# Delta rule: a chunk's preparation moved to the end of the step before, and VectorE's side work moved between two marks of each level

## The chip, the cores and the metric

One Trainium2 chip, one of its cores. The program is one launch that computes a whole two-part network block. The metric is device microseconds of one execution; a run's figure is the median of several executions.

## What is computed

The kernel is a long chain of stages (a first block with three mixers and a feed-forward, then two layers with retrieval of experts). The change touches one stage alone, the gated delta rule of the first of these two layers. Cut to what matters, per chunk and head, in both directions of time:

```python
def step(S, inp):                      # one chunk of one head
    qc, kc, vc, gc, bc = inp
    gc = jnp.cumsum(gc, axis=-1)
    decay = jnp.exp(jnp.where(incl, gc[..., :, None] - gc[..., None, :], -jnp.inf))
    kk = jnp.einsum('bhid,bhjd->bhij', kc, kc)
    a = eye + jnp.where(strict, kk * decay * bc[..., :, None], 0.0)
    sol = lax.linalg.triangular_solve(a, rhs, left_side=True, lower=True, unit_diagonal=True)
    u, w = sol[..., :dv], sol[..., dv:]
    v_new = u - w @ S
    o = (qc * jnp.exp(gc)) @ S + (incl * (qc @ kc.T) * decay) @ v_new
    S = S * jnp.exp(g_last) + (kc * jnp.exp(g_last - gc)).T @ v_new
    return S, o
```

There are 16 value heads of width 128 and 512 positions (256 of the context, 256 of the sequence). At the end each head's output is normalized by its root mean square and multiplied by a gain.

## The kernel before, in words

**Work.** The kernel takes chunks of 128 positions and four heads at a time: four groups of heads by four chunks are 16 pieces, k = 0 to 15. A piece is a tile of 128 by 512 (four heads side by side). Both directions are held in one matrix per head, forward below the diagonal, backward above. For each piece there are three jobs:

- **Preparation** (`pe_prep`, `act_prep`, `pool_prep`, `dve_prep`). Two DMAs bring rows of cumulated gates (E and F). ScalarE subtracts them from the column (`differences`, 4 instructions for each direction, L2027), VectorE takes the larger (`pr.min`, L2052), ScalarE the exponential, TensorE four small products of k and q into a bank (`pr.k`, L2007 and L2008), VectorE multiplies (`dve_products`, L2076 for AT, L2078 for the other). GpSimd masks AT to blocks of 8 (`prod`, L2042). VectorE sums them (L2085 through the helper L221) and scales and spreads them (L2089, L2093, `dve_block`); TensorE sends them to all partitions (L2015, `in.ab`); VectorE inverts the 8 by 8 blocks by substitution (`dve_substitute`: seven pairs of L2107 and L2109 in parts 0 to 2; part 3 is L2113, L2114 and L2118, the first W).
- **Inverse** (`pe_inverse`, `act_inverse`, `pool_inverse`, `dve_inverse`): four levels double the block from 8 to 128. A level is transpose W (PE L2134), R = masked transpose (DVE L2165, two halves), y = N R (PE L2142), T = scaled copy (ACT L2185, four heads), x = T B (PE L2150), W = W - x (DVE L2171, two halves). N and B are masked copies that GpSimd makes (L2197, L2204). After the last level GpSimd cuts W into two triangles (L2229, `in.XT`).
- **Recurrence** (`pe_recur` and so on): carry (DVE L2338, four instructions a direction, after PE L2291), vn (PE L2300), its copies on ScalarE, the output (PE L199, added by DVE L2346 or copied by ACT), the state (PE L2321, DVE L2356 or L2353), and for the last piece of a group the norm (DVE L2361 and L2362, one pair per chunk). `pool_stage` does triangles (L2229), Q (L2259) and the scaled v (L2264) a step ahead of it.

**Order.** Each engine has a program of its own, in order, written by hand with semaphores. `chunks` runs 18 steps; in step k the inverse of piece k, the preparation of piece k+1, the stage work of k-1 and the recurrence of k-2 stand side by side. Each of these is a generator with 13 rounds, r = 0 to 12, and `paced` takes one round of each in turn, the inverse first. Rounds 3n, 3n+1 and 3n+2 hold level n: the transpose and R are in the first, y and T in the second, x and W in the third; round 12 holds no level. So whatever an engine is given in round 3n stands behind R there, and whatever it is given in round 3n+2 stands behind W and ahead of the next R. The z projection (`pe_zstep`, L2459: eight matmuls of 512 columns a step, spread by the table `Z`) fills TensorE beside them; its result is copied out by ScalarE in round 12 and stored by the SP queue, which then issues the rows for Q (`sp_queries`, L1962).

**Banks.** The eight PSUM banks go round in a queue (`Banks`): `take` hands out the bank that was given back longest ago and waits for what was named when it was given back.

**VectorE before.** Preparation: r 1 `pr.min`; r 4 and 5 the two products; r 6 and 7 the block work; r 9 to 12 the four parts of the substitution. Recurrence: r 1 and 2 the two carries; r 5 and 6 the outputs; r 7 and 8 the states; for the last piece of a group norms in r 3, 4, 11 and 12. An instruction made with `v()` waits for the preceding one of its engine.

A piece with `st` = (k-2) % 4 = 0 in the recurrence has no carry, one with `st` = 3 has no state but the norms; outputs are added on VectorE at `st` 1 and 3. In steps of k % 4 = 2, 3, 0, 1 the recurrence is at `st` 0, 1, 2, 3.

## Time and profile before

| | |
|---|---|
| median of 3 runs | 4194.38 us (4189.41 to 4195.66) |
| the profiled execution's own time | 4192.27 us |
| its span in the profile | 4190.5 us |
| busy: PE, DVE, ACT, POOL | 83%, 63%, 32%, 29% of the span |
| steps 0 to 15 of the delta rule | 1264.27 to 1760.49 us, 496.2 us |
| its first W ready, its end | 1264.27 us, about 1794.4 us |

Times inside the trace are counted from the start of the span. "DVE" is VectorE, "ACT" ScalarE, "POOL" GpSimd, "PE" TensorE. A step is counted here from the end of one L2118 (the first W of a piece) to the end of the next; the four levels and the last part of the substitution for the next piece lie in it.

### The profile page before, as it was taken

What the parts mean: (1) busy time and instruction counts of PE and PEld (TensorE: products, weight loads), DVE (VectorE), ACT (ScalarE), POOL (GpSimd) and SP (SyncE); (2) the same over time, 40 slices, a digit from 0 to 9 for tenths busy, and PEclk for the clock granted to TensorE, in tenths of its full rate; (3) what the DMA queues carried; (4) which work ended last, traced back from release to release, by engine and by line L of the source; (5) the groups of instructions that cost most, each with busy time, mean ns of one, the idle gap of its engine ahead of it and who ended that gap; (6) DMA issues with size and microseconds to landing.
All of it is one profiled execution on the core that took longest, in us unless ns stands there. A gap on an engine that the chain in (4) does not pass through costs nothing.

```text
span 4190.5 us, 38888 instructions
## 1 busy us (share of the span) xinstructions
PE 3490.2 (83%) x11382; PEld 1850.7 (44%) x11382; DVE 2644.0 (63%) x5552; ACT 1356.8 (32%) x3747; POOL 1210.7 (29%) x1228
## 2 busy tenths in 40 slices
PE   7888978999877888879989887877788787877877
PEld 2344435844335666666544432322233365322222
DVE  3756454858766776545788469677555445887444
ACT  1232120003433455412334333433333232433333
POOL 0001100000005565502343433433444101443332
PEclk9889989999989999989999999999999998999999
DMA  5523314653421112055999999999999714999998
GB/s 219 201 81 137 125 63 169 222 199 134 190 82 33 53 57 62 23 231 201 407 399 409 399 414 419 402 421 421 408 414 420 289 62 175 416 421 408 418 421 362
DMA packets 169765, 1088.29 MB, mean 260 GB/s; under 512 B 16432, under 2 KB 45488, under 8 KB 51152
## 3 DMA queue, kind: packets, MB, share of 16 engines
q0 software_dynamic: 112608, 820.04, 47.7%
q1 hardware_dynamic: 56944, 265.77, 17.2%
q8 instruction: 90, 1.47, 0.1%
q14 instruction: 123, 1.01, 0.1%
HBM read 1075.19 MB, written 10.55 MB: 259 GB/s over the span
## 4 chain that ended last, share of the span: by engine, by line
PE 31%; DVE 27%; DMA 18%; issue 12%; POOL 7%; ACT 4%; DVEq 0%; POOLq 0%; ACTq 0%; SPq 0%
PE bank L199 20%; DMA arena<-in_uv,arena 16%; POOL arena L3023 6%; DVE arena L3040 6%; ACT arena L211 3%; PE bank L2991 3%; DVE arena L443 2%; PE bank L1620 2%; DVE arena L561 2%; DVE arena L217 1%; DVE arena L2109 1%; DVE arena L221 1%; PE bank L2459 1%; DMA arena<-in_w_rows 1%; DVE arena L216 1%
## 5 line engine op out<-in xcount | busy, mean ns | idle before, releaser
L2991 PE MATMUL bank<-arena 128*128 128x512 f32 x3072 | 1491.2, 620 | 353.3 <-ACT arena L211 350.6
L211 ACT ACTIVATE arena<-arena 128x1 f32<-128x1 f32 (+5 forms) x2639 | 872.5, 331 | 2003.9 <-DVE arena L3040 1127.7
L199 PE MATMUL bank<-arena 128*128 128x256 f32 (+4 forms) x4640 | 1299.3, 439 | 73.1 <-ACT arena L211 36.1
L3040 DVE CUSTOM_DVE_ANT_0 arena<-arena 128x1024 f32<-128x1024 f32 x768 | 942.0, 1227 | 609.5 <-DMA arena<-in_uv,arena 571.2
L3023 POOL DMA_INDIRECT arena<-in_uv,arena x768 | 794.9, 1035 | 1251.0 <-PE bank L2991 812.5
L2991 PEld LDWEIGHTS bank<-arena 128*128 128x128 f32 x3072 | 547.5, 192 | 1269.5 <-ACT arena L211 818.6
L199 PEld LDWEIGHTS bank<-arena 128*128 128x128 f32 (+2 forms) x4640 | 804.1, 195 | 556.5 <-issue 427.3
L211 ACT ACTIVATE arena<-bank 128x512 f32<-128x512 f32 (+4 forms) x306 | 160.7, 525 | 481.4 <-PE bank L199 322.6
L443 DVE CUSTOM_DVE_ANT_0 arena<-arena 128x1024 f32<-128x1024 f32 x192 | 240.7, 1254 | 33.9 <-DMA arena<-in_w_rows 22.3
L626 POOL TENSOR_SCALAR arena<-arena 128x1 f32<-128x1 f32 (+3 forms) x48 | 16.9, 351 | 664.7 <-ACT arena L211 471.1
L561 DVE SCALAR_TENSOR_TENSOR arena<-bank,arena 128x508 f32<-128x508 f32 (+2 forms) x248 | 159.0, 641 | 8.8
L211 ACT ACT_TABLE_LOAD x92 | 118.0, 1283 | 78.1 <-DMA arena<-gates_rest 26.3
L217 DVE TENSOR_SCALAR arena<-bank,arena 128x256 f32<-128x256 f32 (+3 forms) x162 | 84.0, 519 | 90.0 <-PE bank L520 48.3
L2185 ACT ACTIVATE arena<-bank,arena 128x128 f32<-128x128 f32 x256 | 73.0, 368 | 208.4 <-PE bank L2142 208.0
L2459 PE MATMUL bank<-arena 128*128 128x512 f32 x256 | 130.2, 611 | 0.0
L2204 POOL TENSOR_TENSOR arena<-arena 128x512 f32<-128x512 f32 x64 | 81.3, 1270 | 91.9 <-DVE arena L2171 46.7
L216 DVE TENSOR_SCALAR arena<-bank,arena 128x256 f32<-128x256 f32 (+5 forms) x98 | 55.4, 565 | 81.0 <-PE bank L199 63.2
L2197 POOL TENSOR_TENSOR arena<-arena 128x512 f32<-128x512 f32 x64 | 81.3, 1270 | 54.2 <-PE bank L2142 50.4
L2171 DVE TENSOR_TENSOR arena<-arena,bank 128x256 f32<-128x256 f32 x128 | 48.2, 418 | 76.3 <-PE bank L2150 72.6
L221 DVE TENSOR_REDUCE arena<-arena 128x32 f32<-128x512 f32 (+10 forms) x99 | 66.2, 669 | 40.2 <-ACT arena L211 34.7
L2134 PE MATMUL bank<-arena 128*128 128x128 f32 x256 | 43.7, 293 | 55.0 <-DVE arena L2118 52.4
L1620 PE MATMUL bank<-arena 128*128 128x512 f32 x176 | 77.4, 602 | 2.7 <-DVE arena L1638 2.7
(255 smaller groups left out, 2599.3 us busy)
## 6 DMA issues: line engine op xcount, KB each, us to landing
arena<-in_w_rows SPq DMA_DIRECT2D x50, 1024.0 KB, 5.0
arena<-in_w_in SPq DMA_DIRECT2D x16, 2048.0 KB, 7.9
arena<-in_wq SPq DMA_DIRECT2D x14, 2048.0 KB, 8.4
arena<-in_dn_w SPq DMA_DIRECT2D x12, 2048.0 KB, 10.0
arena<-in_w_up SPq DMA_DIRECT2D x11, 2048.0 KB, 8.0
arena<-in_dn_wo SPq DMA_DIRECT2D x8, 2048.0 KB, 11.2
arena<-in_w_rows POOLq DMA_DIRECT2D x14, 1024.0 KB, 6.1
arena<-decay_rest SPq DMA_DIRECT2D x56, 256.0 KB, 5.0
```

Of the source, the lines that this page charges most:

```text
L199: t = p.e.matmul(out, l, r, start=(i == 0), stop=(i == n - 1))
L211: return a().activation(out, in_, f, **kw)
L216: return v().tensor_scalar(out, a, s1, None, op0)
L217: return v().tensor_scalar(out, a, s1, s2, op0, op1)
L221: return v().tensor_reduce(out, a, AX, op)
L443: v().tensor_tensor_reduce(trash, w[:, j, :], self.crow[r], 1.0, 0.0, ALU.mult, ALU.add, self.M[m][:, j0 + j, c:c + 1]).then_inc(*(V.up("m ...
L561: t = v().scalar_tensor_tensor(dst[:, :, o], src[:, :, f], wc(d + h), dst[:, :, o], ALU.mult, ALU.add)
L1620: t = p.e.matmul(bs[n], m["act"][:, 4 * c + k, 128 * i:128 * i + 128], ch[:, k, 512 * half:512 * half + 512], start=(c + k == 0), stop=(4 ...
L2459: t = p.e.matmul(b, self.hT[:, q, 128 * i:128 * i + 128], m["zch"][:, q, :], start=(q == 0), stop=(q == 7))
L2991: t = p.e.matmul(by[half], m["dg"][ee % 4], m["uv"][r][:, 1024 + 512 * half:1536 + 512 * half], start=(ee == 0), stop=(ee == 127))
L3023: g.e.indirect_dma_start(out=m["uv"][q % 7], out_offset=None, in_=self.I["uv"], in_offset=bass.IndirectOffsetOnAxis(ap=m["idx"][n % 2][:, ...
L3040: v().tensor_tensor_reduce(self.spare, uv[:, 0:1024], m["ht"][n % 2], 1.0, 0.0, ALU.mult, ALU.add, m["acts"][:, ee:ee + 1]).then_inc(*V.up ...
```

## The change

No arithmetic is added or removed; instructions change their round, and one norm pair its step.

- `pe_prep`: the products of piece k+1 (`pr.k`) move from r 3 of their own preparation to r 11 of the preparation before it, so one step earlier; their bank is given back at r 5 instead of r 6. The `in.ab` matmul moves from r 8 to r 6.
- `act_prep`: the differences move from r 0 to r 8 and 9 of the preparation before; the exponential from r 2 to r 0.
- `pool_prep`: `prod` moves from r 5 to r 1, and in `pool_chunks` the preparation goes ahead of the stage work within a round.
- `dve_prep`: `pr.min` moves to r 12 of the preparation before, behind the first W; products to r 0 and 4; the block work to r 4; substitution parts to r 7, 10, 10 and 12.
- `dve_recur`: both carries in r 1, both outputs in r 6, states in r 7 and 10, the norms of chunks 0 and 1 in r 7 and 10, those of chunks 2 and 3 in r 1 of the next step (`st` 0 of the next group), for the last group in r 12.
- `Z`: one z matmul less in r 9, one more in r 12; for the steps with k % 4 > 0 those of r 0, 6 move to r 2, 3.

```diff
     def pe_prep(self, p, m, k):
...
+            if r == 0 and k == 0:
+                products(0)
+            if r == 5:
+                self.banks.give(("pr.k", k), V.of("pr.P", k))
             if r == 6:
-                self.banks.give(("pr.k", k), V.of("pr.P", k))
-            if r == 8:
                 p.wait_ge(*V.of("in.Z", k))
...
-            if r == 12:
+            if r == 11:
                 self.banks.give(("in.ab", k), V.of("in.sub", k))
+                if k < 15:
+                    products(k + 1)
...
     def act_prep(self, a, m, k):
...
             if r == 0:
+                if k == 0:
+                    differences(0, 0)
+                    differences(0, 1)
                 a.wait_ge(*self.V.of("pr.min", k))
                 act(a, E, E, ACT.Exp, scale=-1.0).then_inc(*self.A.up("pr.e", k))
+            if r in (8, 9) and k < 15:
+                differences(k + 1, r - 8)
...
     def pool_prep(self, g_, m, k):
         for r in range(self.ROUNDS):
-            if r == 5:
+            if r == 1:
...
     def dve_prep(self, v, m, k):
...
+            if r == 0:
+                if k == 0:
+                    larger(0)
+                self.dve_products(v, m, k, 0)
+            if r == 4:
+                self.dve_products(v, m, k, 1)
+                for part in range(3):
+                    self.dve_block(v, m, k, part)
             if r == 7:
-                self.dve_block(v, m, k, 2)
-            if r > 8:
-                self.dve_substitute(v, m, k, r - 9)
+                self.dve_substitute(v, m, k, 0)
+            if r == 10:
+                self.dve_substitute(v, m, k, 1)
+                self.dve_substitute(v, m, k, 2)
+            if r == 12:
+                self.dve_substitute(v, m, k, 3)
+                if k < 15:
+                    larger(k + 1)
...
         for r in range(self.ROUNDS):
-            if r in (1, 2) and st > 0:
-                carry(r - 1)
-            if r in (5, 6) and self.second_visit(k, r - 5):
-                output(r - 5)
-            if r in (7, 8) and st < 3:
-                state(r - 7)
-            if st == 3 and r in (3, 4, 11, 12):
-                norm({3: 0, 4: 1, 11: 2, 12: 3}[r])
+            for d in range(2):
+                if r == 1 and st > 0:
+                    carry(d)
+                if r == 1 and st == 0 and g > 0:
+                    norm(g - 1, 2 + d)
+                if r == 6 and self.second_visit(k, d):
+                    output(d)
+                if r == (7, 10)[d]:
+                    if st < 3:
+                        state(d)
+                    else:
+                        norm(g, d)
+                if r == 12 and k == 15:
+                    norm(g, 2 + d)
...
-    Z = ({6: 1, 7: 1, 8: 1, 9: 2, 10: 1, 11: 1, 12: 1}, {0: 1, 6: 1, 8: 1, 9: 2, 10: 1, 11: 1, 12: 1})
+    Z = ({6: 1, 7: 1, 8: 1, 9: 1, 10: 1, 11: 1, 12: 2}, {2: 1, 3: 1, 8: 1, 9: 1, 10: 1, 11: 1, 12: 2})
...
-            (self.pool_inverse(g, m, k), k < 16), (self.pool_stage(g, m, k - 1), 0 < k < 17),
-            (self.pool_recur(g, m, k - 2), k > 1), (self.pool_prep(g, m, k + 1), k < 15)))
+            (self.pool_inverse(g, m, k), k < 16), (self.pool_prep(g, m, k + 1), k < 15),
+            (self.pool_stage(g, m, k - 1), 0 < k < 17), (self.pool_recur(g, m, k - 2), k > 1)))
```

## Rows read from the trace of the kernel before

**Rows 1.** Stages by windows: steps 0-2, first and third group of four, step 15, step 10.

```profile
core 0: us, PE busy (x) PEld busy (x) DVE busy (x) ACT busy (x) POOL busy (x), PEclk, DMA share, GB/s
1264.27:1347.14 82.87, 67.27 (x366) 48.45 (x366) 53.48 (x128) 31.42 (x93) 47.85 (x43) 0.95 0.11 29
1347.14:1476.73 129.59, 109.50 (x656) 85.06 (x656) 92.17 (x211) 64.25 (x199) 76.64 (x70) 0.96 0.17 54
...
1606.17:1735.15 128.98, 109.68 (x656) 85.76 (x656) 92.15 (x211) 62.30 (x193) 76.63 (x70) 0.95 0.16 49
1735.15:1760.49 25.34, 24.13 (x159) 20.07 (x160) 11.60 (x28) 11.86 (x36) 14.77 (x13) 1.00 0.07 21
1574.03:1606.17 32.14, 27.64 (x154) 21.45 (x154) 18.95 (x44) 15.21 (x43) 18.96 (x17) 0.91 0.09 28
```

**Rows 2.** Timeline, step 1: one level in which nothing stands in the way.

```profile
start us, us, engine line op out<-in xcount [idle before <-releaser]
1297.83 0.76 DVE L2165 TENSOR_TENSOR arena<-bank,arena 128x256 f32<-128x256 f32 x2 [0.53 <-PE bank L2134]
1298.52 1.06 PE L2142 MATMUL bank<-arena 128*128 128x128 f32 x8
1299.62 1.14 ACT L2185 ACTIVATE arena<-bank,arena 128x128 f32<-128x128 f32 x4 [2.93 <-PE bank L2142]
1301.34 0.75 DVE L2171 TENSOR_TENSOR arena<-arena,bank 128x256 f32<-128x256 f32 x2 [1.92 <-PE bank L2150]
```

**Rows 3.** Timeline, step 7, second level: carry behind W, and TensorE's fill.

```profile
1484.63 1.51 DVE L2338 SCALAR_TENSOR_TENSOR arena<-bank,arena 128x128 f32<-128x128 f32 x4
1486.19 1.16 PE L2300 MATMUL bank<-arena 128*128 128x128 f32 x8 [0.31 <-DVE arena L2338]
1486.24 0.76 DVE L2165 TENSOR_TENSOR arena<-bank,arena 128x256 f32<-128x256 f32 x2
1488.08 1.95 PE L199 MATMUL bank<-arena 128*128 128x128 f32 x16
1490.96 0.75 DVE L2171 TENSOR_TENSOR arena<-arena,bank 128x256 f32<-128x256 f32 x2 [3.14 <-PE bank L2150]
```

**Rows 4.** VectorE's groups by line, 1509.98 to 1639.42 (busy us, mean ns, idle before).

```profile
L2109 DVE TENSOR_TENSOR arena<-arena 128x56 f32<-128x56 f32 (+6 forms) x28 | 14.3, 510 | 1.0
L2165 DVE TENSOR_TENSOR arena<-bank,arena 128x256 f32<-128x256 f32 x32 | 12.1, 420 | 9.6 <-PE bank L2134 9.0
L2171 DVE TENSOR_TENSOR arena<-arena,bank 128x256 f32<-128x256 f32 x32 | 12.0, 418 | 16.7 <-PE bank L2150 15.7
L2338 DVE SCALAR_TENSOR_TENSOR arena<-bank,arena 128x128 f32<-128x128 f32 x24 | 8.4, 351 | 4.3 <-PE bank L2291 3.2
L2107 DVE TENSOR_TENSOR arena<-bank,arena 128x56 f32<-128x56 f32 (+6 forms) x28 | 5.4, 192 | 1.0
L2052 DVE TENSOR_TENSOR arena<-arena 128x512 f32<-128x512 f32 x4 | 4.8, 1204 | 0.5
```

**Rows 5.** Timeline, end of step 8: from the last level to the next piece's first transpose.

```profile
1537.51 1.34 POOL L2229 TENSOR_SCALAR_AFFINE_SELECT arena<-arena 128x512 f32<-128x512 f32 x2 [1.88 <-DVE arena L2171]
1537.68 0.49 DVE L2109 TENSOR_TENSOR arena<-arena 128x16 f32<-128x16 f32 x1
1538.91 0.19 DVE L2113 TENSOR_TENSOR arena<-arena 128x32 f32<-128x32 f32 x1
1539.36 0.69 DVE L2118 TENSOR_TENSOR arena<-arena 128x512 f32<-128x512 f32 x1
1540.14 1.28 POOL L2204 TENSOR_TENSOR arena<-arena 128x512 f32<-128x512 f32 x1 [1.29 <-DVE arena L2118]
```

**Rows 6.** Timeline, step 9, last level: a VectorE instruction beside one of GpSimd.

```profile
1566.11 1.26 POOL L2197 TENSOR_TENSOR arena<-arena 128x512 f32<-128x512 f32 x1
1566.27 1.15 DVE L2109 TENSOR_TENSOR arena<-arena 128x24 f32<-128x24 f32 x1
```

**Rows 7.** DMA issues of the page: rows of gates, KB each, median us to landing.

```profile
arena<-decay_rest SPq DMA_DIRECT2D x56, 256.0 KB, 5.0
```

More of the change, by code:

```diff
@@ L2000, in pe_prep, with products @@
         P, V = self.P, self.V
-        g, c = divmod(k, 4)
-        for r in range(self.ROUNDS):
-            if r == 3:
-                b = self.banks.take(p, "pr.k", k)
-                for u in range(2):
-                    kT, qT = (m[n][:, 2 * g + u, H4[c]] for n in ("kT", "qT"))
-                    p.e.matmul(b[:, H4[u]], kT, kT, start=True, stop=True)
-                    t = p.e.matmul(b[:, H4[2 + u]], kT, qT, start=True, stop=True)
-                t.then_inc(*P.up("pr.k", k))
+        def products(k):
+            g, c = divmod(k, 4)
+            b = self.banks.take(p, "pr.k", k)
+            for u in range(2):
+                kT, qT = (m[n][:, 2 * g + u, H4[c]] for n in ("kT", "qT"))
+                p.e.matmul(b[:, H4[u]], kT, kT, start=True, stop=True)
+                t = p.e.matmul(b[:, H4[2 + u]], kT, qT, start=True, stop=True)
+            t.then_inc(*P.up("pr.k", k))
+        for r in range(self.ROUNDS):
+            if r == 0 and k == 0:
+                products(0)
+            if r == 5:
+                self.banks.give(("pr.k", k), V.of("pr.P", k))
             if r == 6:
-                self.banks.give(("pr.k", k), V.of("pr.P", k))
-            if r == 8:
                 p.wait_ge(*V.of("in.Z", k))
@@ L2015, in pe_prep, with differences @@
                 p.e.matmul(b, m["block"], m["prod"], start=True, stop=True).then_inc(*P.up("in.ab", k))
[L2016 removed]
+            if r == 11:
                 self.banks.give(("in.ab", k), V.of("in.sub", k))
+                if k < 15:
+                    products(k + 1)
             yield
     def act_prep(self, a, m, k):
[L2021 removed]
+        def differences(k, d):
+            x, (g, c) = (m["F"][k % 2] if d else m["E"][k % 4]), divmod(k, 4)
+            a.wait_ge(*self.D.of(f"pg{d}{'ab'[k % 2]}.in", k))
+            for h in range(4):
+                t = (a() if h == 0 else a.e).activation(x[:, H4[h]], x[:, H4[h]], ACT.Identity,
+                                                       bias=m["GC"][:, d, c, 4 * g + h:4 * g + h + 1], scale=-1.0)
+                t.then_inc(*(self.A.up("pr.d", k, d) if h == 3 else self.A.up("pr.dh")))
+        E = m["E"][k % 4]
         for r in range(self.ROUNDS):
             if r == 0:
[L2024 to L2030 removed]
+                if k == 0:
+                    differences(0, 0)
+                    differences(0, 1)
                 a.wait_ge(*self.V.of("pr.min", k))
                 act(a, E, E, ACT.Exp, scale=-1.0).then_inc(*self.A.up("pr.e", k))
+            if r in (8, 9) and k < 15:
+                differences(k + 1, r - 8)
             yield
@@ L2356, in state, with norm @@
             v().tensor_tensor(S, S, b, ALU.add).then_inc(*V.up("re.S", k, d))
-        def norm(c):
+        def norm(g, c):
             ob = heads(m["ob"][c], 4)
@@ L2364, in dve_recur @@
         for r in range(self.ROUNDS):
-            if r in (1, 2) and st > 0:
-                carry(r - 1)
-            if r in (5, 6) and self.second_visit(k, r - 5):
-                output(r - 5)
-            if r in (7, 8) and st < 3:
-                state(r - 7)
-            if st == 3 and r in (3, 4, 11, 12):
-                norm({3: 0, 4: 1, 11: 2, 12: 3}[r])
+            for d in range(2):
+                if r == 1 and st > 0:
[11 more added lines that the diff above has]
+                    norm(g, 2 + d)
             yield
```

22 lines of the change are left out of this document (4 added, 18 removed).

## Prediction

> **What bounds the stage now.** Read first the windows [rows 1]. A group of four steps takes 129.3 us (129.59 the first, 128.98 the last of three), and no engine is full in it: PE 109.6 us by a count that overlaps its matmuls, DVE 92.1, POOL 76.6, ACT 64. So a chain through several engines sets the pace, and the question is what lengthens that chain.
>
> Then one level that nothing disturbs [rows 2]: R starts 0.53 us after the W before it, y, T and x follow, W starts 3.51 us after R began and takes 0.75. That is 0.53 + 3.51 + 0.75 = 4.79 us, so four levels would take 19.2 us. A step takes 32.3 us (129.3 / 4), 2.6 of it its last part [rows 5]. So the levels last 7.4 us on average and not 4.8.
>
> Where the rest goes is seen in the second level of step 7 [rows 3]. The carry of one direction stands behind W; the transpose is long done, and R starts only at 1486.24, when the carry (1.51 us) is over. TensorE's vn needs the same carry (idle 0.31), y stands behind vn, the 1.95 us of L199 stand between y and x, and DVE then waits 3.14 us for x. So DVE works when the chain needs it and idles when it doesn't. By group [rows 4]: of DVE's 129.3 - 92.1 = 37.2 us of idleness, 9.0 + 15.7 + 3.2 = 27.9 end with a TensorE result; the other 9.3 are gaps between its 210 instructions.
>
> The end of a step [rows 5]: after the last W come two pairs of the substitution (0.49 us for the L2109 there), L2113, L2114 and L2118; the triangles start right behind that W, at 1537.51, and the next piece's B at 1540.14, 2.6 us later.
>
> **The change, part by part.** The count of instructions is the same on every engine, so only order and overlap change. I therefore add up DVE's queue for one group, since every R and W of the chain is in it.
>
> 1. *DVE's own work:* 92.1 busy + 9.3 gaps = 101.4 us.
> 2. *Idleness that the chain forces.* Between W and R DVE now has nothing to do in three levels of four: 12 x 0.53 = 6.4 us. In the first level the maximum for the piece after next (`pr.min`) stands there, its exponential on ACT is done before R is; 4 x 0.1 = 0.4. The sum is 108.2, so 21.1 us a group could go.
> 3. *Does PE keep up?* In the second level it issues z, vn, y, o and x. With the 0.2 us taken off that a group's end overlaps the next, vn, y, x and z (as many columns) take 0.9 each and o 1.8 [rows 2, 3], 5.4 together: W can start 5.6 us after the W before, a level of 6.4. DVE has R, a product, the sum over blocks, four small instructions and W there, 5.4 us undisturbed. That is 1.0 us a level on PE's side, covered as soon as DVE loses 1 us to item 4; in the other levels DVE has more to do than PE. The carries of both directions now delay W of the first level: 0.83 (maximum) + 0.75 + 0.8 + 3.1 + 0.1 + 0.75 = 6.4 us instead of 4.8. That is inside item 1; it is why the levels don't come down to 4.8 us [rows 2].
> 4. *GpSimd beside DVE.* This is the term that I can't read off. An L2109 that starts 0.16 us after a GpSimd multiplication ends 0.05 us after it and takes 1.15 us [rows 6]. Its partner L2107, same width, one operand in a bank, takes 0.19 on average [rows 4]. L2109 loses 14.3 - 5.4 = 8.9 us a group and `pr.min` (1.20 against the 0.69 of L2118, same shape) 2.0; with the block work, norms and copy it is some 14 us. All two-operand DVE work now stands where GpSimd makes N, B, Q, V2. Added: L2113, L2114 and L2118 now run beside the triangles (1.34 us [rows 5]), +1.1 a step, 4.4; norms of chunks 2 and 3 now stand beside `prod`, triangles and N, up to 1.27 + 0.64 + 0.64 + 1.27 less what they pay today, +3; block work +0.5 a step, 2; substitution pairs beside B, V2 twice and N, +0.7 a step, 2.8. Taken off: `pr.min` is now issued before GpSimd's B, -2.0. Sum +10.2. The bounds are -11 (the losses of the two rows vanish) and +36 (below); I take a value near the measured mean, 0.3 us per instruction.
>
> So a group takes 108.2 + 10.2 = 118.4, and 129.3 - 118.4 = 10.9 us go; three groups 32.7. Steps 0 to 2 and 15 [rows 1] hold little recurrence: the pairs of substitution leave the end of the step (-0.4 each), and their third and fourth levels, now 6 to 7.4, lose the work behind W; I take 2 us each, 8 in all, between 0 and 12.
>
> **What is moved past queues.** The differences (eight ACT instructions ahead of the first T now) go between the third and fourth T, where ACT has little else; their DMAs are issued a step ahead and land 5.0 us after issue [rows 7]. `prod` ahead of the triangles on GpSimd delays these by 1.3 us; they are needed in round 4. The products leave PE's second level (0.9) and fill its end, together with a second z matmul in round 12: 3.5 us behind the last x, against 3.2 (the end of x, W, and the 2.2 us that item 4 leaves for the last part) and what DVE is late with that W, 1 us or more. I count nothing; without that cover 0.3 to 0.9 a step. SP stores z and issues the rows for Q only after z's last matmul, now about 1 us later in the step. Bank waits: with the products' bank held over the step's end, y of the third level takes the bank of the first output, and the last transpose that of the second; both are added right behind R, in time. Steps without recurrence: nothing. After the stage, the output projection starts earlier by the same amount, its weights are loaded behind the last z, and so moves with it.
>
> **TensorE's clock.** Step 10 [rows 1] has a granted clock of 0.91 and step 15 one of 1.00, so part of the former runs at 1.2 GHz and not 2.4. Shorter idle ends of steps should keep it at the upper level more often; I count nothing for it. Lower clock in a first level would make PE its bound and cost up to 1.4 us a step.
>
> **Sum.** 32.7 + 8 = 41 us. The profiled execution took 4192.3 us: 4152. The median of the runs is 2.1 us (0.05%) above it, which I leave out. A difference under 0.2%, 8.4 us, I call no change; that is about what a measurement of this kernel can tell.
>
> **Rivals.**
>
> *A, strict turns.* Wherever GpSimd has work queued, it and DVE take turns: every two-operand DVE instruction waits out the rest of one GpSimd instruction, and the next of GpSimd then goes ahead. Worked through the levels: in the second, AC waits for Q's and N's multiplications (+2.3), in the last four L2109 each let one through (6.7 us instead of 4.8), the norms add 3.8, the end of a step is 2.2. Group 123 to 126; 3 x (3.3 to 6.3) + 8 is 18 to 27 us, so 4165 to 4174. For it: two L2109 beside GpSimd, 1.15 and 0.49 us [rows 5, 6]. Against: the mean loss of an L2109 today is 0.32 us, so most don't wait long. Chance 0.17. The Trainium skill, "SBUF — State Buffer", section "SBUF: two separate sides", has this rule: VectorE instructions with two SBUF inputs and GpSimd's share a port pair as an exclusive lock for a whole instruction. By that rule, the trace agrees for the single instruction [rows 6].
>
> *B, nothing added.* The instructions fall into GpSimd's gaps (it idles 53 us a group) and no more is lost than today: 3 x 21.1 + 8 = 71, with 1 us of PE's side a step 60: 4121 to 4132. Chance 0.12.
>
> *C, ACT late.* The exponentials of Q stand ahead of the copies of vn, and their rows are issued later; T of the second level then comes 1 to 2.5 us late in three steps of four, or T of the last behind the differences. 3 x 3 x 1 to 2.5 is 9 to 22 us given back: 4161 to 4174. For it: 5.0 us to landing; against: ACT is busy 64 of 129 us and T takes 1.14 of a level of 6.4 [rows 1, 2]. Chance 0.12.
>
> *D, slower.* GpSimd's N and B come late because DVE holds it up as well, and each of a group's 72 DVE instructions with two SBUF operands (28 L2109 among them) waits. The free 21.1 us are used up at (14 + 21) / 72 = 0.49 us each, from there on the kernel is slower. At 0.7 us it is 50 - 14 = +36 a group, 3 x 15 - 8 = +37 us: 4229. For it: everything is packed into windows of 3 to 4 us in which GpSimd works. Chance 0.09.
>
> The forecast has 0.50, 4138 to 4165. The range takes in half of B, A and C: 4127 to 4180. Faster by over 0.2%: 0.50 + 0.17 + 0.12 and a part of C lower, 0.83; same 0.08 (the ends of A and C and a mild D); slower 0.09.
>
> **What would show it.** In the changed kernel: R behind each W at about 0.5 us with no L2338 between (item 2); idle before L2171 for L2150 far below 15.7 us a group, under 5 (items 1, 3); L2109's mean at 0.5 to 0.7 us, `pr.min` at 0.7 (item 4); 2.2 us from the last W to the next first transpose; a group at 118 us. Wrong would be: T waiting on ACT's own queue (C), a mean of L2109 over 0.8 with N or B ending idle time of PE (D), or DVE's waits for x unchanged, which would say that PE and not DVE's order set the pace.

## The result, and the profile after

| | before | after |
|---|---|---|
| median, over 5 runs of each on one chip | 4194.38 us (4189.41 to 4196.24) | 4175.06 us (4167.43 to 4177.66) |
| ratio after to before, 95% interval | | 0.995, 0.9938 to 0.9961 |
| the profiled execution's own time | 4192.27 us | 4176.0 us |
| its span | 4190.5 us | 4174.3 us |
| first W to last W (steps 0 to 15) | 496.2 us | 483.0 us |

The change makes the kernel faster by 0.5%, 19 us by the medians and 16 by the two profiled executions. The forecast was 41 us, 4152. The direction is right, and the forecast size is more than twice the measured one.

The page of the profile after: its span, and the busy time by engine.

```profile
span 4174.3 us, 38907 instructions
...
PE 3489.0 (84%) x11382; PEld 1845.0 (44%) x11382; DVE 2684.9 (64%) x5552; ACT 1356.8 (33%) x3747; POOL 1216.6 (29%) x1228
```

The count of instructions is the same on every engine. DVE's busy time was 2644.0 us in the page of before, so it is 40.9 us busier with the same work. The rest of the kernel hardly moved: from 34 us behind the last W to the end of the span it is 2394.8 us, against 2396.0.

The windows of the stage after, cut at the end of a first W as in [rows 1]: steps 0 to 2, three groups of four, step 15.

```profile
core 0: us, PE busy (x) PEld busy (x) DVE busy (x) ACT busy (x) POOL busy (x), PEclk, DMA share, GB/s
1262.51:1348.62 86.11, 72.27 (x366) 52.33 (x366) 59.70 (x129) 32.49 (x96) 47.39 (x43) 0.86 0.11 25
1348.62:1475.47 126.85, 110.82 (x656) 84.77 (x656) 105.93 (x211) 64.25 (x198) 76.47 (x70) 0.96 0.17 55
1475.47:1599.39 123.92, 108.10 (x656) 82.18 (x656) 102.79 (x211) 64.25 (x198) 78.26 (x70) 0.99 0.18 56
1599.39:1722.45 123.06, 106.08 (x648) 80.20 (x648) 102.74 (x210) 61.71 (x190) 78.27 (x70) 1.00 0.17 53
1722.45:1745.51 23.06, 23.01 (x157) 19.45 (x158) 11.59 (x28) 11.85 (x36) 14.78 (x13) 1.00 0.10 30
```

The groups take 126.9, 123.9 and 123.1 us, 2.7, 5.5 and 5.9 less than before; 10.9 less was forecast for each. Steps 0 to 2 take 3.2 us more, with a granted clock of 0.86 where it was 0.95 [rows 1], and step 15 takes 2.3 less. DVE's busy time in the second group is 102.8 us; in the first it is 105.9.

VectorE's groups by line in that second group, to be read beside [rows 4]; columns as there.

```profile
L2129 DVE TENSOR_TENSOR arena<-arena 128x56 f32<-128x56 f32 (+6 forms) x28 | 12.2, 437 | 1.0
L2185 DVE TENSOR_TENSOR arena<-bank,arena 128x256 f32<-128x256 f32 x32 | 12.1, 419 | 8.4 <-PE bank L2154 8.0
L2191 DVE TENSOR_TENSOR arena<-arena,bank 128x256 f32<-128x256 f32 x32 | 12.0, 418 | 1.8 <-PE bank L2170 0.3
...
L2113 DVE TENSOR_TENSOR arena<-arena 128x256 f32<-128x256 f32 x8 | 7.2, 905 | 0.3
L2063 DVE TENSOR_TENSOR arena<-arena 128x512 f32<-128x512 f32 x4 | 6.8, 1712 | 0.5
L2138 DVE TENSOR_TENSOR arena<-arena 128x512 f32<-128x512 f32 x5 | 6.1, 1217 | 0.2
...
L2381 DVE TENSOR_TENSOR arena<-arena 128x512 f32<-128x512 f32 x4 | 4.3, 1068 | 0.3
...
L2376 DVE TENSOR_TENSOR arena<-arena,bank 128x512 f32<-128x512 f32 x4 | 2.8, 688 | 2.2 <-PE bank L2341 1.8
...
L2373 DVE COPY arena<-bank 128x512 f32<-128x512 f32 x2 | 1.4, 692 | 1.1 <-PE bank L2341 1.0
```

W (now L2191) waits 0.3 us a group for x, where it waited 15.7 [rows 4]. The chain's idleness on DVE has gone as forecast. What remains is the turn from W to R (8.0, at L2185) and the wait for s (1.8 at L2376, 1.0 at L2373). Against that, the maximum L2063 now takes 1.71 us on average; it took 1.20 [rows 4], and 0.7 was forecast.

The end of step 6 and the start of step 7, timeline of the kernel after:

```profile
1474.31 1.17 DVE L2138 TENSOR_TENSOR arena<-arena 128x512 f32<-128x512 f32 x1
...
1475.56 1.27 POOL L2224 TENSOR_TENSOR arena<-arena 128x512 f32<-128x512 f32 x1 [0.63 <-DVE arena L2138]
...
1475.61 1.77 DVE L2063 TENSOR_TENSOR arena<-arena 128x512 f32<-128x512 f32 x1
...
1477.48 0.76 DVE L2185 TENSOR_TENSOR arena<-bank,arena 128x256 f32<-128x256 f32 x2
...
1478.05 1.13 PE L2162 MATMUL bank<-arena 128*128 128x128 f32 x8 [1.00 <-DVE arena L2185]
...
1479.22 1.14 ACT L2205 ACTIVATE arena<-bank,arena 128x128 f32<-128x128 f32 x4 [1.18 <-PE bank L2162]
```

This is where a large part of the gain was lost. The first W (L2138) ends at 1475.48. GpSimd's B (L2224) starts 0.08 us behind it, the maximum 0.13 us behind it. Then the maximum runs 1.77 us and not 0.69, and R comes 2.00 us behind W. In the forecast R came at 0.83. It is the same in 13 of the 15 steps that prepare another: the maximum starts 0.13 us behind W and takes 1.75 to 1.78 us; in steps 10 and 14 it takes 1.55.

A table of all steps, worked out from the timelines, shows the same for the whole stage. Each column is a sum over the 16 steps of the time from one W to the next; "end" is the part from the last W of a step to the next first W.

| kernel | level 1 | 2 | 3 | 4 | end | stage |
|---|---|---|---|---|---|---|
| before | 105.5 | 111.0 | 112.4 | 118.6 | 48.6 | 496.2 |
| after | 126.3 | 113.9 | 113.9 | 99.5 | 29.4 | 483.0 |

The fourth level and the end gave 38.3 us. The first level took 20.8 of them back, the second and third another 4.4. Which part of this is the maximum's is the question of the first experiments.

### The profile page after: what moved, and what is told of

Same layout as the page of the kernel before. It is cut to its first block, busy times and chain, and to the rows that moved or that the text cites. A ratio compares the mean times of both kernels' runs of the same rounds, so it can differ in the third digit from the quotient of the medians.

```text
span 4174.3 us, 38907 instructions
## 1 busy us (share of the span) xinstructions
PE 3489.0 (84%) x11382; PEld 1845.0 (44%) x11382; DVE 2684.9 (64%) x5552; ACT 1356.8 (33%) x3747; POOL 1216.6 (29%) x1228
## 4 chain that ended last, share of the span: by engine, by line
PE 34%; DVE 29%; DMA 18%; issue 10%; POOL 6%; ACT 4%; DVEq 0%; POOLq 0%; SPq 0%; ACTq 0%
PE bank L199 20%; DMA arena<-in_uv,arena 16%; DVE arena L3066 6%; PE bank L3017 5%; POOL arena L3049 5%; ACT arena L211 3%; DVE arena L443 2%; PE bank L1620 2%; DVE arena L561 2%; DVE arena L217 1%; DVE arena L221 1%; DVE arena L2129 1%; DMA arena<-in_w_rows 1%; DVE arena L216 1%; PE bank L2154 1%
## 5 line engine op out<-in xcount | busy, mean ns | idle before, releaser
L3017 PE MATMUL bank<-arena 128*128 128x512 f32 x3072 | 1489.4, 619 | 355.5 <-ACT arena L211 352.5
L3017 PEld LDWEIGHTS bank<-arena 128*128 128x128 f32 x3072 | 546.7, 192 | 1270.5 <-ACT arena L211 822.1
L2485 PE MATMUL bank<-arena 128*128 128x512 f32 x256 | 127.8, 601 | 0.0
L2205 ACT ACTIVATE arena<-bank,arena 128x128 f32<-128x128 f32 x256 | 73.0, 368 | 117.8 <-PE bank L2162 117.0
L2224 POOL TENSOR_TENSOR arena<-arena 128x512 f32<-128x512 f32 x64 | 81.2, 1269 | 87.1 <-DVE arena L2191 68.4
L2162 PE MATMUL bank<-arena 128*128 128x128 f32 x512 | 73.3, 289 | 17.7 <-DVE arena L2185 16.9
L2162 PEld LDWEIGHTS bank<-arena 128*128 128x128 f32 x512 | 67.0, 202 | 37.4 <-issue 29.3
L2170 PE MATMUL bank<-arena 128*128 128x128 f32 x512 | 72.6, 287 | 10.7 <-ACT arena L2205 9.7
## 6 DMA issues: line engine op xcount, KB each, us to landing
arena<-in_dn_w SPq DMA_DIRECT2D x12, 2048.0 KB, 10.1
```

The costliest lines, as they stand in the source:

```text
L2162: t = p.e.matmul(b[:, H4[h]], m["N"][:, H4[h]], m["R"][:, H4[h]], start=True, stop=True)
L2485: t = p.e.matmul(b, self.hT[:, q, 128 * i:128 * i + 128], m["zch"][:, q, :], start=(q == 0), stop=(q == 7))
L3017: t = p.e.matmul(by[half], m["dg"][ee % 4], m["uv"][r][:, 1024 + 512 * half:1536 + 512 * half], start=(ee == 0), stop=(ee == 127))
```

## The experiments

The theory: the maximum and B are released by the same W and need the same thing, so whoever starts first holds the other up for its whole length; the maximum loses because it starts 0.05 us later. The rivals: the first level is long for another reason (both carries in it, TensorE's work there), and then a cheap maximum gives nothing; or TensorE sets the pace, and less work on it gives time. Ratios are to the kernel before, with their 95% intervals. The stage's sums of all runs stand in one table behind the experiments. Each sum is read from one profiled execution, and what lies outside of the stage varied between 3686 and 3701 us in these, so a few us in the stage need not show in the kernel's time.

### Who starts first behind the first W

One wait more on GpSimd lets B (third level of the inverse, behind the first W) start behind the maximum:

```diff
             g.wait_ge(*V.of("in.W", k, l - 1))
+            if l == 3 and k < 15:
+                g.wait_ge(*V.of("pr.min", k + 1))
```

> The changed kernel, but GpSimd's first B of a step (L2224) also waits for the maximum of the step after (pr.min), so the maximum behind the first W meets no GpSimd multiplication. Theory M (the maximum waits out B, 1.77 us instead of 0.69, and R stands behind it): the maximum takes 0.69, R starts 0.9 us after the first W instead of 2.0, the first level is 1.1 us shorter in 15 steps, 12 to 18 us less than the changed kernel's 4175: 4157 to 4163. Theory P (TensorE or another engine sets the pace of the first level and the order on VectorE matters little): the maximum takes 0.69, but later waits take its place, under 5 us gained. Theory N (B then comes late for x): x of the first level waits for GpSimd, no gain or a loss.

Measured: 4162.4 us, 0.9919 (0.9906 to 0.9933), which does not overlap with the kernel after. The same place in its timeline (GpSimd's lines are two further down, since the edit adds two):

```profile
1466.08 1.35 POOL L2251 TENSOR_SCALAR_AFFINE_SELECT arena<-arena 128x512 f32<-128x512 f32 x2 [1.38 <-DVE arena L2191]
1466.26 0.51 DVE L2134 TENSOR_TENSOR arena<-arena 128x32 f32<-128x32 f32 x1
1466.80 1.17 DVE L2138 TENSOR_TENSOR arena<-arena 128x512 f32<-128x512 f32 x1
...
1468.10 0.69 DVE L2063 TENSOR_TENSOR arena<-arena 128x512 f32<-128x512 f32 x1
...
1468.90 0.75 DVE L2185 TENSOR_TENSOR arena<-bank,arena 128x256 f32<-128x256 f32 x2
1468.93 1.28 POOL L2226 TENSOR_TENSOR arena<-arena 128x512 f32<-128x512 f32 x1 [1.51 <-DVE arena L2063]
```

The maximum takes 0.69 us and R starts 0.93 us behind W. The first levels sum to 111.5 us and not 126.3; the second to fourth and the end are within 1.5 us of the kernel after. So the placing of one instruction, not its amount of work, was worth 16.6 us of the stage, 12.7 us of the kernel's median. In steps 10 and 14 nothing changes: GpSimd starts B only 3.1 us behind W there, whoever waits, and the maximum takes 1.55 us beside the masked copy N in both kernels.

The second form adds no wait. It only moves DVE's two waits for ScalarE's differences ahead of the last substitution pairs, so that nothing stands between the first W and the maximum:

```diff
             if r == 12:
+                for d in range(2 if k < 15 else 0):
+                    v.wait_ge(*self.A.of("pr.d", k + 1, d))
                 self.dve_substitute(v, m, k, 3)
```

> The changed kernel; only VectorE's waits for ScalarE's differences, which stood between the first W (L2138) and the maximum (L2063), now stand ahead of the substitution's last part. The maximum then starts 0.04 us after the first W instead of 0.13, and GpSimd's B starts 0.09 us after it. If the one that starts first goes ahead (theory M with the rule of turns), the maximum takes 0.7 us, B is held up by it instead, R starts 0.83 us after the first W, and the gain is that of the run in which B waited for the maximum: 4160 to 4164. If GpSimd goes ahead whoever starts first, the maximum still takes 1.8 us: 4173 to 4177.

Measured: 4166.69 us, 0.992 (0.9906 to 0.9933), above the 4160 to 4164 that I expected; the kernel before was slower too beside this run (4199.15, against 4195.09 beside the first experiment), so by ratio both forms gain the same. Its timeline, DVE's and GpSimd's lines two further down (L2063 stands ahead of the edit and keeps its number):

```profile
1466.91 1.34 POOL L2251 TENSOR_SCALAR_AFFINE_SELECT arena<-arena 128x512 f32<-128x512 f32 x2 [1.38 <-DVE arena L2193]
1466.96 0.62 DVE L2135 TENSOR_TENSOR arena<-arena 128x32 f32<-128x32 f32 x1
1467.62 0.67 DVE L2136 TENSOR_TENSOR arena<-arena 128x32 f32<-128x32 f32 x1
...
1468.32 0.69 DVE L2140 TENSOR_TENSOR arena<-arena 128x512 f32<-128x512 f32 x1
...
1469.05 0.69 DVE L2063 TENSOR_TENSOR arena<-arena 128x512 f32<-128x512 f32 x1
...
1469.10 1.77 POOL L2226 TENSOR_TENSOR arena<-arena 128x512 f32<-128x512 f32 x1 [0.85 <-DVE arena L2140]
...
1469.84 0.76 DVE L2187 TENSOR_TENSOR arena<-bank,arena 128x256 f32<-128x256 f32 x2
```

W ends at 1469.01. Now the maximum starts 0.04 us behind it and B 0.09, and the durations have changed places: 0.69 for the maximum and 1.77 for B. The work of both is what it was, and 0.05 us of start time decide which of them takes 1.77. This settles the mechanism: two semaphore waits between W and the maximum delayed it by about 0.09 us (0.13 against 0.04), though what they wait for had been done for 3.5 to 8.2 us. In 12 of 15 steps the maximum now takes 0.69, and the first level of most of them falls from 7.72 to 6.55 us; in steps 6, 10 and 14 it takes 1.00, 1.65 and 1.00.

The moved waits are not free where they stand now. They follow the last W, which also releases the triangles (L2251), and the first of the two short additions (L2135) starts 0.05 us behind these: it takes 0.62 us where it took 0.19, and the second (L2136) 0.67 where it took 0.51. The end of a step grows from 1.97 to 2.18 us in most steps, 2.3 us over the stage (29.4 to 31.7). It is the same effect once more.

### Each part alone

The kernel before with the changed kernel's order of the recurrence on DVE, all else as before:

```diff
-            if r in (1, 2) and st > 0:
-                carry(r - 1)
-            if r in (5, 6) and self.second_visit(k, r - 5):
-                output(r - 5)
-            if r in (7, 8) and st < 3:
-                state(r - 7)
-            if st == 3 and r in (3, 4, 11, 12):
-                norm({3: 0, 4: 1, 11: 2, 12: 3}[r])
+            for d in range(2):
+                if r == 1 and st > 0:
+                    carry(d)
+                if r == 1 and st == 0 and g > 0:
+                    norm(g - 1, 2 + d)
+                if r == 6 and self.second_visit(k, d):
+                    output(d)
+                if r == (7, 10)[d]:
...
```

> The kernel before with the new order of the recurrence on VectorE alone (carries in r 1, outputs in r 6, states in r 7 and 10, norms in r 7, 10 and r 1 of the next step); preparation as before. Theory M (VectorE's place between R and W is worth what it takes off the way from W to R): the second level loses the 1.2 us that R waited there in most steps and the steps with k % 4 = 1 lose 3.1 us at their end, while the first level gains what the second carry adds (about 1.0 us): 5 to 20 us faster than before, 4175 to 4190. Theory P (TensorE sets the pace): no change, 4194.

Measured: 4221.23 us, 1.0058 (1.0045 to 1.007), slower than both kernels and outside of what I expected (4175 to 4190). The first level of step 8 in its timeline:

```profile
1523.97 0.69 DVE L2118 TENSOR_TENSOR arena<-arena 128x512 f32<-128x512 f32 x1
...
1525.62 1.91 PE L2291 MATMUL bank<-arena 128*128 128x256 f32 x4
1525.87 0.76 DVE L2165 TENSOR_TENSOR arena<-bank,arena 128x256 f32<-128x256 f32 x2 [1.21 <-PE bank L2134]
...
1527.57 1.51 DVE L2338 SCALAR_TENSOR_TENSOR arena<-bank,arena 128x128 f32<-128x128 f32 x4 [0.95 <-PE bank L2291]
...
1529.54 1.51 DVE L2338 SCALAR_TENSOR_TENSOR arena<-bank,arena 128x128 f32<-128x128 f32 x4 [0.46 <-PE bank L2291]
...
1531.18 0.69 DVE L2052 TENSOR_TENSOR arena<-arena 128x512 f32<-128x512 f32 x1
...
1531.98 0.75 DVE L2171 TENSOR_TENSOR arena<-arena,bank 128x256 f32<-128x256 f32 x2
```

Both carries now stand ahead of W, and DVE waits for their matmuls (0.95 and 0.46 us idle, L2291) with the maximum of the old preparation behind them. W comes 8.1 us behind the first W, where it took 5.6 before. The first levels sum to 130.9 us (before 105.5), the fourth to 136.2 (118.6): state and old substitution now share that level, and in steps 5, 9 and 13 R waits 3.2 to 3.9 us there for its transpose (1.7 before); the cause of that wait stays open.

The reverse, the kernel after with the old order of the recurrence on DVE:

```diff
-            for d in range(2):
-                if r == 1 and st > 0:
-                    carry(d)
...
+            if r in (1, 2) and st > 0:
+                carry(r - 1)
+            if r in (5, 6) and self.second_visit(k, r - 5):
+                output(r - 5)
+            if r in (7, 8) and st < 3:
+                state(r - 7)
...
```

> The changed kernel with the recurrence's order of before: preparation moved, carries, outputs, states and norms where they were. Theory M: R of the first level still stands behind the maximum, which waits for B (2.0 us), and behind W of the first level the second carry still delays R (1.2 us): as slow as before or slower, 4185 to 4205. Theory P: as the changed kernel, 4175.

Measured: 4189.3 us, 0.9985 (0.9976 to 0.9994). The stage takes 493.4 us, 2.8 less than before; its second levels sum to 142.7, since the carry of one direction stands behind W again and the block work stands in the same level. So the stage gains 2.8 us with one half, loses 32.5 with the other, and gains 13.2 with both. The halves are not to be had separately: each vacates the rounds that the other fills.

### The maximum in the window between R and W

The kernel after with the maximum in round 0 of its own preparation, behind R, and the first part of the products in round 1:

```diff
             if r == 0:
-                if k == 0:
-                    larger(0)
+                larger(k)
+            if r == 1:
                 self.dve_products(v, m, k, 0)
...
-                if k < 15:
-                    larger(k + 1)
```

> The changed kernel, but the maximum of a piece stands behind the first R of its step and its first product behind the carries. Theory M: R starts 0.5 us after the first W, the maximum takes 0.7 to 0.9, the first W is 0.7 us earlier; but prod on GpSimd starts only at 6 us into the step and N of the second level behind it at about 9, so y of the second level waits for GpSimd 1 to 2 us: between 4170 and 4195, and in the profile the first level near 7.0 and the second near 9. Theory P: as the changed kernel, 4175.

Measured: 4188.45 us, 0.9983 (0.9974 to 0.9992). The maximum is cheap there (0.70 us on average) and the first levels drop to 111.1, but the second and third grow to 128.8 and 120.1. The wait that appears is TensorE's for GpSimd's N: ahead of y (L2160) it is idle for 38.1 us in 26 waits until N (L2215) is there, where the kernel after has 1.3 us in 2. The exponential, the product and `prod` come later, and N behind them on GpSimd, as I had expected before the run. Here an early maximum is worth more than a cheap one; both together need its place behind the first W and its start ahead of B.

### The triangles

GpSimd's triangles (L2251 in the first experiment's timeline) start right behind the last W, at 1466.08 there, and beside them L2134 takes 0.51 us and the first W 1.17; undisturbed these are 0.19 and 0.69. This edit puts them behind B of the next step's first level. In its own run, and together with B behind the maximum:

```diff
+        def cut(k):
+            g.wait_ge(*V.of("in.W", k, 6))
...
                 tri(3)
+                if k:
+                    cut(k - 1)
...
-            if r == 12:
+            if r == 12 and k == 15:
+                cut(k)
```

> The changed kernel, but GpSimd cuts the triangles of a piece behind the first B of the next step instead of ahead of it, so that L2133, L2134 and L2138 (both, both, first W) run beside nothing. Theory M: from the last W to the next first W 1.3 us instead of 1.97, 0.65 us in each of 15 steps, 10 us; the maximum still waits for B. Given back in part if prod comes later (GpSimd has triangles ahead of it, up to 3.9 us into the step against 3.7 now). 4163 to 4170. Theory P: under 3 us.

> Both edits of the two runs before. Theory M: their gains add up, unless prod and N of the second level now come late on GpSimd (B, triangles, prod, triangles, N in a row are 6.7 us from 0.9 on, N done at 7.6 and wanted at about 7.4 by y of the second level): 20 to 27 us under the changed kernel, 4148 to 4155. Theory P: no more than 5 us.

Measured: 4172.04 us, 0.9941 (0.9928 to 0.9955) alone; 4156.5 us, 0.9911 (0.9898 to 0.9925) together. Both lie above what I expected (4163 to 4170, and 4148 to 4155), and the first is not set apart from the kernel after, although its stage is 10.0 us shorter in the profiled execution. The end of a step falls from 1.97 to 1.18 us in most steps, 10.7 over the stage (29.4 to 18.7). With both edits, the second levels grow by 8.3 us over those of the first experiment (114.5 to 122.8), so of the 10.2 us at the end only 4.9 remain in the stage (466.4 to 461.5): the triangles now hold up the block work, whose Z (L2113) takes 10.1 us in the second group of steps and 7.2 in the first experiment. The step from 0.9919 to 0.9911 lies inside the intervals.

One triangle behind B and the other in round 5, to spread them:

```diff
+                if k:
+                    cut(k - 1, 1)
+            if r == 5 and k:
+                cut(k - 1, 0)
```

> As the run with both edits (B behind the maximum, triangles behind B), but of the triangles only the one of the backward direction stands behind B, the other in r 5. In the run with both edits the second level was 8.07 us instead of 7.3, by theory M because prod and N of the second level came late behind two triangles. Theory M: the second level returns to 7.3 to 7.5 or 0.65 us under 8.07, 6 to 10 us under that run's 4156.5: 4147 to 4151. Theory P: no difference, 4156.

Measured: 4155.55 us, 0.9901 (0.9888 to 0.9914), no gain over the pair that the intervals set apart, and outside of what I expected (4147 to 4151). In step 7 the second level falls to 6.70 us (8.07 with both triangles behind B), but the third, where the other triangle now stands, is 7.90 instead of 7.05.

Last, the same edit of the triangles as above (behind B, `cut(k - 1)` in round 0) on the kernel with the waits of the maximum moved up, and without the added wait:

> The same, and the triangles behind B as in the earlier run of that edit. If first come goes first: the last part 1.2 us instead of 1.97, the maximum 0.7: 4153 to 4160, as the run with both edits. Otherwise as the run with the triangles behind B alone, 4172.

Measured: 4152.94 us, 0.9887 (0.9872 to 0.9902). It has the lowest ratio of all, just below the 4153 to 4160 us that I expected, and beats both kernels; from the two versions with the triangles moved and B behind the maximum its interval does not set it apart. The groups of its second group of four steps (lines two further down):

```profile
L2131 DVE TENSOR_TENSOR arena<-arena 128x56 f32<-128x56 f32 (+6 forms) x28 | 14.8, 530 | 1.0
...
L2115 DVE TENSOR_TENSOR arena<-arena 128x256 f32<-128x256 f32 x8 | 10.1, 1262 | 0.3
```

L2115, the block work's Z, takes 1262 ns and not 905 as in the kernel after, and L2131 takes 530 and not 437: DVE pays 5.5 us a group elsewhere for the short end. In the three places tried, what the triangles cost moved with them and did not vanish.

### Does TensorE set the pace?

Six of the eight products of each z matmul are left out, so z has two eighths of its sum; all else stays. In the kernel after, in the one before, and in that of the first experiment:

```diff
-                t = p.e.matmul(b, self.hT[:, q, 128 * i:128 * i + 128], m["zch"][:, q, :], start=(q == 0), stop=(q == 7))
+                if q in (0, 7):
+                    t = p.e.matmul(b, self.hT[:, q, 128 * i:128 * i + 128], m["zch"][:, q, :], start=(q == 0), stop=(q == 7))
```

> The changed kernel, in which six of eight matmuls of the z projection are left out (z then lacks 6/8 of its sum): 5.2 us less for TensorE in each of 16 steps, 83 us. Theory M (VectorE's queue is the chain now): nearly nothing, the last level and the steps' ends unchanged, 0 to 15 us faster: 4160 to 4175. Theory P (TensorE's own work is the chain): 40 to 80 us faster.

> The kernel before with the same six of eight z matmuls left out (z then lacks 6/8 of its sum). In the changed kernel this gave only 4 us. If TensorE's own work was part of the chain before (item 3 and the waits of VectorE for y and x), the kernel before gains more, 10 to 30 us: 4165 to 4185. If VectorE's order was the chain there too (theory M), under 5 us: 4190 to 4194.

> The run in which B waits for the maximum (4162.4), with the same z matmuls left out. Theory M: VectorE's queue is still the chain, under 6 us gained: 4156 to 4162. If TensorE has become the next bound once the maximum is out of the way: 10 us or more, under 4152.

Measured: after 4171.35 us, 0.9938 (0.9923 to 0.9954), where the whole kernel after has 0.995; before 4191.82, 0.9999 (0.9989 to 1.0009); first experiment 4157.38, 0.9917 (0.9901 to 0.9934), where it had 0.9919 whole. Nowhere is there a gain that the intervals set apart. A window of 125 us in the middle of the stage, the kernel before with few z products first:

```profile
core 0: us, PE busy (x) PEld busy (x) DVE busy (x) ACT busy (x) POOL busy (x), PEclk, DMA share, GB/s
1470.00:1595.00 125.00, 92.08 (x596) 77.46 (x594) 87.56 (x203) 64.25 (x198) 74.92 (x69) 0.92 0.18 55
```

and the kernel after with few z products:

```profile
1470.00:1595.00 125.00, 97.49 (x612) 81.30 (x612) 104.34 (x213) 65.49 (x202) 78.12 (x71) 0.92 0.18 56
```

TensorE's busy time fell to 92.1 and 97.5 of 125 us, but so did the granted clock, to 0.92; in the same window it is 0.96 in the whole kernel before and 0.99 in the whole kernel after. In the kernel before, the first levels even grew, from 105.5 to 119.4 us, and the clock fell in them and in the ends of the steps: its mean over the 16 first levels is 0.72, against 0.86, and over the ends 0.79, against 0.96. The first level of step 4, the whole kernel before and then the one with few z products, columns as above:

```profile
1380.41:1386.00 5.59, 5.34 (x38) 4.80 (x38) 4.37 (x9) 2.94 (x10) 3.81 (x4) 1.00 0.74 253
...
1380.19:1387.53 7.34, 7.28 (x37) 6.76 (x38) 3.60 (x10) 2.40 (x6) 4.24 (x4) 0.67 1.00 382
```

TensorE is busy nearly throughout in both, with 38 and 37 matmuls; the level at a clock of 0.67 lasts 1.75 us longer (DMA traffic is higher in it too, which no run separates). So "less work on TensorE gives nothing" is shown, but in the kernel before it is no proof that TensorE's work is off the chain, since the lower clock took back a part that these runs don't separate. For the kernels after it agrees with the 0.3 us that W waits for x.

### The stage in all runs

Sums as in the first table, and the mean duration of the maximum.

| kernel | level 1 | 2 | 3 | 4 | end | stage | maximum |
|---|---|---|---|---|---|---|---|
| before | 105.5 | 111.0 | 112.4 | 118.6 | 48.6 | 496.2 | 1.07 |
| after | 126.3 | 113.9 | 113.9 | 99.5 | 29.4 | 483.0 | 1.67 |
| B behind the maximum | 111.5 | 114.5 | 113.2 | 98.1 | 29.3 | 466.4 | 0.81 |
| waits moved up | 110.3 | 114.5 | 113.7 | 99.9 | 31.7 | 470.0 | 0.79 |
| recurrence alone | 130.9 | 103.8 | 118.5 | 136.2 | 39.3 | 528.7 | 0.76 |
| preparation alone | 104.8 | 142.7 | 106.7 | 98.2 | 40.9 | 493.4 | 1.70 |
| maximum behind R | 111.1 | 128.8 | 120.1 | 104.6 | 29.4 | 494.1 | 0.70 |
| triangles behind B | 124.9 | 114.8 | 113.2 | 101.3 | 18.7 | 473.0 | 1.68 |
| both | 110.1 | 122.8 | 110.3 | 99.2 | 19.1 | 461.5 | 0.80 |
| triangles apart, B behind | 109.1 | 114.8 | 115.7 | 102.8 | 19.7 | 462.0 | 0.75 |
| waits moved up, triangles | 107.5 | 122.0 | 109.8 | 102.4 | 19.9 | 461.6 | 0.75 |
| few z, after | 128.1 | 113.1 | 108.6 | 101.9 | 29.2 | 480.9 | 1.54 |
| few z, before | 119.4 | 112.3 | 110.5 | 108.9 | 50.5 | 501.6 | 0.85 |
| few z, B behind | 115.9 | 112.4 | 108.7 | 101.5 | 29.2 | 467.7 | 0.73 |

## Why the prediction was right in direction and wrong in size

The sum had three groups at 118.4 us and 8 us at the edges. The second group came out at 123.9, of which 102.8 are DVE's work (forecast 102.3), 9.6 small gaps (9.3) and 11.6 larger idleness (6.8). Two steps of the prediction failed. In the kernel the larger is one term of item 4, which had the maximum's cost with the wrong sign; in the sum it is hidden, since other terms of the item erred the other way. What the sum of this group shows as missing is item 2, 4.8 of the 5.5 us.

**Item 1 and the idleness that was to go: right.** DVE's count and its small gaps are the same, and the waits for x fell from 15.7 to 0.3 us a group.

**Item 4, the first step that failed: "`pr.min` is now issued before GpSimd's B, -2.0".** It was read off the order in the code, as if the first W released only DVE. The same W releases B, the maximum has two more waits to pass, and B starts first. Measured: over the stage the maximum's loss (duration less 0.69) went from 6.1 to 15.7 us, which is 9.6 / 4 = +2.4 us a group. So the term was off by 4.4 us a group, 13 for three. The first experiment puts a price on it from the other side: with the maximum first the groups take 121.8, 120.2 and 119.8, that is 12.0 us less for the three, and the steps 0 to 2 take 4.6 less. Together this is 16.6 of the 28 us between the forecast and the stage's measured 13.2.

The other terms of item 4, as losses a group by the same count: the end of a step +2.9 (forecast 4.4), norms +2.1 (3), block work +3.9 (2), substitution with the copy ahead of it -0.5 (+2.8). All of the item came to +10.7 in the second group (102.8 less 92.1), against +10.2. That its sum is right is luck: the parts err in both directions. The substitution pairs already stood beside GpSimd's instructions before the change, and they lost no more where they stand now; the mean of L2129 is 0.44 us, below the 0.5 to 0.7 that the prediction gave as its sign (0.51 before).

The norms of chunks 2 and 3 at the start of step 10, timeline after:

```profile
1570.39 1.26 POOL L2224 TENSOR_TENSOR arena<-arena 128x512 f32<-128x512 f32 x1 [0.17 <-POOL arena L2249]
...
1570.80 1.41 DVE L2381 TENSOR_TENSOR arena<-arena 128x512 f32<-128x512 f32 x1
...
1571.80 1.54 POOL L2053 TENSOR_TENSOR arena<-arena 128x512 f32<-128x512 f32 x1
...
1572.24 1.64 DVE L2382 SCALAR_TENSOR_TENSOR arena<-arena 128x512 f32<-128x512 f32 x1
...
1573.47 1.94 POOL L2249 TENSOR_SCALAR_AFFINE_SELECT arena<-arena 128x512 f32<-128x512 f32 x2
...
1573.92 1.00 DVE L2381 TENSOR_TENSOR arena<-arena 128x512 f32<-128x512 f32 x1
...
1574.95 1.00 DVE L2382 SCALAR_TENSOR_TENSOR arena<-arena 128x512 f32<-128x512 f32 x1
```

Four instructions of 0.69 us undisturbed take 5.05 us, 2.3 more. Where both engines have work queued, they do take turns here. The first level of these steps takes 9.48 to 10.08 us where it took 7.8 to 8.0.

**Item 2, the second step that failed, short by 4.8 us a group.** It had only the turn from W to R, 12 at 0.53, and 0.4 for the exponential. The turns measure 8.0 and not 6.4: four of the twelve are 0.74 to 1.42 us, since, as I read it, TensorE still had other matmuls ahead of the transpose. And the term had no wait for s, which now stands alone in the window between R and W:

```profile
1521.77 0.76 DVE L2185 TENSOR_TENSOR arena<-bank,arena 128x256 f32<-128x256 f32 x2 [0.53 <-PE bank L2154]
...
1523.29 1.03 PE L2341 MATMUL bank<-arena 128*128 128x256 f32 x4
...
1524.35 0.69 DVE L2376 TENSOR_TENSOR arena<-arena,bank 128x512 f32<-128x512 f32 x1 [1.82 <-PE bank L2341]
```

R ends at 1522.53, s (L2341) lands at 1524.32, and DVE has nothing else for 1.82 us; the window of the group has 2.8 us of this. With 1.6 for the turns, 0.3 for x and 0.1 more ahead of the first product these are the 4.8 us. Moving work out of a place took away what used to hide the wait there. I had costed only the waits of the chain.

**Item 3, does TensorE keep up: right.** W waits 0.3 us a group for x, and taking matmuls away gave nothing, with the reserve on the clock given above.

**The edges, wrong: -8 forecast, +0.9 measured.** Steps 0 to 2 took 3.2 us more. With the maximum first they take 81.5, 1.4 less than before, so most of this is the same step; the granted clock there was 0.86 after and 0.90 in that experiment, against 0.95, and how much the clock took is open. Step 15 gave 2.3, as taken.

**Rivals.** *A* gave 123 to 126 us a group and 4165 to 4174, and the numbers came out next to it: 123.9, 4175. Its mechanism is half right. The turns are seen at the norms. But the last level takes 6.43 us in most steps and not 6.7, and the loss that mattered was not a queue's turn but one start, 0.05 us late. The Trainium skill, "SBUF — State Buffer", section "SBUF: two separate sides", says that whoever starts first holds the shared port pair for the whole instruction; by that rule the runs agree, in both directions: 1.77 us for the maximum behind B, 1.77 us for B behind the maximum. A wait for the whole of the other and then the full 0.69 or 1.27 would be 1.91 us in either case, an estimate from the starts and undisturbed times above, so the rule is some 0.14 us too long here. Had I applied it to the two starts behind the first W, the failed step would have been in doubt. *B* (nothing added) fell with DVE's 40.9 us more. *C* fell as a cost, though a late T does occur: T (L2205 at 1479.22 above) starts 0.04 us behind the last matmul of y, as in nearly all levels, but in the third level of steps 5, 9 and 13 it starts 1.80 us behind it, with ScalarE busy on sums of squares for the norm. DVE's own work put W 0.3 to 1.0 us behind x there, so this cost nothing by itself; W waits for x 0.3 us a group. *D* needed a mean loss of 0.49 us for each of 72 instructions; measured is (14 + 10.7) / 72 = 0.34.

**The clock.** I counted nothing for it. The groups show 0.96, 0.99 and 1.00, up from 0.95 to 0.96, and steps 0 to 2 show 0.86, down from 0.95.

## What to carry to other kernels

When two engines that hold each other up are released by the same instruction, the one with fewer waits in front of it goes first: count the waits between the releaser and the instruction, and put those that are long satisfied ahead of the releaser. Here that moved two waits, added no instruction, and gave 13 us in the stage, as much as the whole change. Look at the new place too: behind another releaser the same two waits lose the same kind of race, here 0.2 us a step. When work is moved out of a window, list every wait that stays in it: what was hidden behind the moved work is paid from then on. And halves of a reordering that fill each other's places can't be judged alone: one half of this one made the kernel slower.

## What the runs showed of the hardware

- A difference of 0.05 us in start decides which of two instructions of 0.69 (DVE) and 1.27 us (GpSimd) runs 1.1 or 0.5 us longer. Between the first W and the maximum lie 0.04 us with no further wait and 0.13 with two waits that are already satisfied, in all 15 steps of either kernel.
- With six of eight z matmuls left out the granted clock of a window of 125 us fell from 0.96 to 0.92 in the kernel before and from 0.99 to 0.92 in the kernel after, and no time was gained. Less work on TensorE is not the same experiment as a faster TensorE.
- Affine selects on GpSimd, the triangles with one input, also hold up a DVE instruction with two: the first W takes 1.17 us beside them and 0.69 without.
